# Norm sums of a GDN layer: from one row per head to one column per 128 tokens, and a page sum copied before the page loads are issued

## What is computed

```python
def l2norm(x):
    return x * lax.rsqrt(jnp.sum(x * x, axis=-1, keepdims=True) + EPS)
...
    q = l2norm(q.reshape(Bn, L, GDN_HEADS, GDN_DK)) * GDN_DK ** -0.5     # 4 heads of 128
    k = l2norm(k.reshape(Bn, L, GDN_HEADS, GDN_DK))
    o, S_new = run_chunks(gdn_chunk, S0, (q, k, v, g, beta), GDN_CHUNK)
    o = rmsnorm(o, norm_g) * jax.nn.silu(z)                              # per head of 128
...
    # fox_sample: softmax over 2048 past rows gathered by page_table, then
    jnp.einsum('bhqk,bkhd->bqhd', p[..., :P], vp)                        # the "page values"
```

## Time and profile before

| | us |
|---|---|
| median of 3 runs | 2619.35 (2618.45 to 2621.92) |
| the profiled execution | 2619.68 |
| its span, first to last instruction | 2617.9 |
| mean granted TensorE clock | 0.977 |

### The profile page before, as it was taken

How to read it: one execution, slowest core, us unless ns; L and a number is a source line. 1 busy time by engine, 2 the same in 40 slices (tenths; PEclk the granted TensorE clock), 3 DMA queues, 4 the chain that set the end, 5 groups by cost and what they waited for, 6 DMA issues and landing times.

```text
span 2617.9 us, 53417 instructions
## 1 busy us (share of the span) xinstructions
PE 2497.5 (95%) x20047; PEld 2395.9 (92%) x20047; DVE 1269.6 (48%) x2225; ACT 566.7 (22%) x847; POOL 1682.8 (64%) x750
## 2 busy tenths in 40 slices
PE   7999998997789899999999999999999899999997
PEld 7999998995467799999999999999889799999996
DVE  4444335786333564443344443366766644444433
ACT  3222101004633222220022220022222221222101
POOL 5777775663411377777777777765545457777773
PEclk9999999998789899999999999999999999999998
DMA  4333334894375333333323333233333423333331
GB/s 125 90 89 96 101 79 113 285 308 131 84 220 188 85 89 95 89 88 99 118 81 89 95 91 100 82 91 100 116 116 98 126 81 88 89 95 90 96 93 61
DMA packets 472390, 291.19 MB, mean 111 GB/s; under 512 B 32785, under 2 KB 438411, under 8 KB 472270
## 3 DMA queue, kind: packets, MB, share of 16 engines
q1 hardware_dynamic: 407286, 221.15, 29.0%
q10 hardware_dynamic: 64992, 68.54, 8.4%
HBM read 273.50 MB, written 16.23 MB: 111 GB/s over the span
## 4 chain that ended last, share of the span: by engine, by line
PE 83%; DVE 8%; ACT 3%; issue 3%; DMA 1%; POOL 1%; ACTq 1%; DVEq 0%; SPq 0%; POOLq 0%
PE ACC L799 72%; PE ACC L1055 2%; PE ACC L1028 1%; DVE TB L2261 1%; DMA SSR<-in_state_ret_S 1%; DVE SSR L2178 1%; POOL WLO L708 1%; PE ACC L1306 0%; PE ACC L1296 0%; DVE XL L1736 0%; PE ACC L1122 0%; PE ACC L1037 0%; POOL WHI L705 0%; PE ACC L893 0%; PE ACC L1330 0%
## 5 line engine op out<-in xcount | busy, mean ns | idle before, releaser
L705 POOL TENSOR_TENSOR WHI<-RAW,ZERO 128x1024 fp32r<-128x1024 f32 (+1 forms) x341 | 693.0, 2032 | 677.2 <-PE ACC L799 640.3
L708 POOL TENSOR_TENSOR WLO<-RAW,WHI 128x1024 fp32r<-128x1024 f32 (+1 forms) x341 | 915.5, 2685 | 49.3 <-POOL WHI L705 2.3
L799 PE MATMUL ACC<-XH,WHI 128*128 128x260 f32 x4032 | 822.6, 285 | 4.3 <-DVE XL L1736 2.0
L799 PE MATMUL ACC<-XH,WLO 128*128 128x260 f32 x4032 | 813.7, 283 | 0.0
L799 PE MATMUL ACC<-XL,WHI 128*128 128x260 f32 x4032 | 812.4, 283 | 0.0
L799 PEld LDWEIGHTS ACC<-XH,WHI 128*128 128x128 f32 x4032 | 624.8, 189 | 22.9 <-issue 6.5
L799 PEld LDWEIGHTS ACC<-XH,WLO 128*128 128x128 f32 x4032 | 622.9, 189 | 0.0
L799 PEld LDWEIGHTS ACC<-XL,WHI 128*128 128x128 f32 x4032 | 621.6, 189 | 0.0
L799 PE MATMUL ACC<-HH,WHI 128*128 128x260 f32 x1408 | 284.2, 283 | 1.1 <-POOL WLO L708 1.1
L799 PE MATMUL ACC<-HH,WLO 128*128 128x260 f32 x1408 | 283.1, 282 | 0.0
L799 PE MATMUL ACC<-HL,WHI 128*128 128x260 f32 x1408 | 282.6, 282 | 0.0
(11 more groups left out here) (391 smaller groups left out, 2398.7 us busy)
## 6 DMA issues: line engine op xcount, KB each, us to landing
RAW<-in_ffn_w_gu SPq DMA_DIRECT2D x176, 512.0 KB, 3.9
RAW<-in_ffn_w_down SPq DMA_DIRECT2D x64, 704.0 KB, 4.8
KPAGES<-in_cache_fox_k ACTq DMA_DIRECT2D x128, 256.0 KB, 4.1
RAW<-in_c_w_in SPq DMA_DIRECT2D x48, 512.0 KB, 3.9
VPAGES<-in_cache_fox_v SPq DMA_DIRECT2D x72, 256.0 KB, 3.1
RAW<-in_ab_w_in SPq DMA_DIRECT2D x28, 512.0 KB, 5.4
VPAGES<-in_cache_fox_v ACTq DMA_DIRECT2D x56, 256.0 KB, 3.3
SSR<-in_state_ret_S ACTq DMA_DIRECT2D x8, 1024.0 KB, 5.4
```

The source lines that it names most:

```text
L705: pool.tensor_tensor(WHI[:, slot, 0:nk, :], RAW[:, slot, 0:nk, :], ZERO[:, :].broadcast_to([P, nk, P]), ALU.add).then_inc(hi_split, 1)
L708: pool.tensor_tensor(WLO[:, slot, 0:nk, :], RAW[:, slot, 0:nk, :], WHI[:, slot, 0:nk, :].bitcast(F32), ALU.subtract).then_inc(split, 1)
L799: ins = pe.matmul(ACC[acc][:, n, 0:HALF], w[:, slot, k, :], a[:, k0 + k, n * HALF:(n + 1) * HALF], start=first and opens, stop=final and c ...
```

## The change

Sums of squares are formed per token. The squares become the weights (128 channels x 128 tokens) and one column of ones is the moving operand, so each matmul gives one column of 128 token sums. 520 tokens make five chunks, the fifth of which is the last 128 tokens (its last 8 are the samples). The result RN is 128 x 40 (8 heads x 5 chunks) for query and key and 128 x 20 for the output norm; root and reciprocal work on that. To come back to channels on partitions, one RN column is broadcast as 128 x 128 weights and multiplied with IDENT, six matmuls a head: 128, 128, 4, 124, 128 and 8 columns, since a chunk that crosses the 260-column halves is cut. ROWSEL and its two memsets go.

DVE instead of ACT squares the queries, before the last fox head's `lo`, and clears bank 7 there; ACT squares the keys in two parts and runs SiLU of values and gates after the roots instead of before. PE runs three of the four page-value turns before the sums. In pair 0 ACT copies page sum 1 before `sample_gates` and before four page loads that it issues, not after them; in both pairs PE runs the two `corner_xt` back to back ahead of the two page turns. KT1 and VT1 move in front of QS, and SQH takes the place from there on.

```diff
-        def row_select(r):
-            return ROWSEL[:, ROWSEL_ONE - r:ROWSEL_ONE - r + NORM_ROWS]
+        CHUNKS = NBLK + 1
+        RN = TA[:, 0:2 * CHUNKS * GDN_HEADS]
+        def chunk_tokens(c):
+            return slice(P * c, P * (c + 1)) if c < NBLK else slice(TOK - P, TOK)
+        def norm_column(c, j):
+            return CHUNKS * GDN_HEADS * (j // GDN_HEADS) + GDN_HEADS * c + j % GDN_HEADS
...
-            pe.wait_ge(fb_dve.sem, fb_dve.value("lo", FOX_HEADS - 1))
             pe.wait_ge(fs_dve.sem, fs_dve.value("norm"))
...
+            def token_sums(b, squares, j):
+                for c in range(CHUNKS):
+                    col = norm_column(c, j)
+                    ins = pe.matmul(bank(b)[:, col:col + 1], squares[:, j, chunk_tokens(c)], ONES[:, 0:1], start=True, stop=True)
+                return ins
+            def over_partitions(acc, j):
+                for c in range(NBLK):
+                    n, first = divmod(P * c, HALF)
+                    col = norm_column(c, j)
+                    left = RN[:, col:col + 1].broadcast_to([P, P])
+                    if first + P <= HALF:
+                        pe.matmul(acc[:, n, first:first + P], left, IDENT[:, :], start=True, stop=True)
+                    else:
+                        cut = HALF - first
+                        pe.matmul(acc[:, n, first:HALF], left, IDENT[:, 0:cut], start=True, stop=True)
+                        pe.matmul(acc[:, n + 1, 0:P - cut], left, IDENT[:, cut:P], start=True, stop=True)
+                n, first = divmod(SEQ, HALF)
+                col = norm_column(NBLK, j)
+                return pe.matmul(acc[:, n, first:first + DEC], RN[:, col:col + 1].broadcast_to([P, P]), IDENT[:, P - DEC:P], start=True, stop=True)
+            for _ in range(V_SLOTS - 1):
+                values()
+            pe.wait_ge(ln_dve.sem, ln_dve.value("sqq"))
             for j in range(2 * GDN_HEADS):
-                for n in range(2):
-                    ins = pe.matmul(ACC[0][0:NORM_ROWS, n, 0:HALF], row_select(r), SQH[:, j, n * HALF:(n + 1) * HALF],
-                                    start=j == 0, stop=j == 2 * GDN_HEADS - 1)
+                if j >= GDN_HEADS:
+                    pe.wait_ge(ln_act.sem, ln_act.value(f"sqk{(j - GDN_HEADS) // 2}"))
+                ins = token_sums(0, SQH, j)
             ln_pe.done(ins, "sum")
-            for _ in range(V_SLOTS):
-                values()
+            values()
+            pe.wait_ge(fb_dve.sem, fb_dve.value("lo", FOX_HEADS - 1))
             pe.wait_ge(ln_dve.sem, ln_dve.value("inv"))
             for j in range(2 * GDN_HEADS):
                 if j >= 2:
                     pe.wait_ge(ln_dve.sem, ln_dve.value(f"mul{j - 2}"))
-                for n in range(2):
-                    ins = pe.matmul(ACC[1 + j % 2][:, n, 0:HALF], IDENT[0:NORM_ROWS, r:r + 1].broadcast_to([NORM_ROWS, P]),
-                                    TA[0:NORM_ROWS, n * HALF:(n + 1) * HALF], start=True, stop=True)
-                ln_pe.done(ins, f"b{j}")
+                ln_pe.done(over_partitions(ACC[1 + j % 2], j), f"b{j}")
...
                 corner_xt(0)
+                corner_xt(1)
                 values()
-                corner_xt(1)
                 values()
...   (output norm: token_sums(0, SQO, j) and over_partitions(ACC[2 + j % 2], j) in the same way)
-            ln_act.done(act.activation(SQH[:, 0:GDN_HEADS, :], channels(GQ, GDN_HEADS), ACT.Square), "sqq")
-            ln_act.done(act.activation(SQH[:, GDN_HEADS:, :], channels(GK, GDN_HEADS), ACT.Square), "sqk")
+            for n in range(2):
+                ln_act.done(act.activation(SQH[:, GDN_HEADS + 2 * n:GDN_HEADS + 2 * n + 2, :], channels(GK + 2 * n, 2), ACT.Square), f"sqk{n}")
+            act.wait_ge(ln_pe.sem, ln_pe.value("sum"))
+            half = CHUNKS * GDN_HEADS
+            for first, c, scale, name in ((0, 1, float(P), "stdq"), (half, 0, 1.0, "stdk")):
+                ln_act.done(act.activation(RN[:, first:first + half], bank(0)[:, first:first + half], ACT.Sqrt, bias=EPSC[:, c:c + 1], scale=scale), name)
             act.wait_ge(cv_pool.sem, cv_pool.value("add3", CONV_CH - 1))
             act.activation(channels(GV, 2 * GDN_HEADS), channels(GV, 2 * GDN_HEADS), ACT.Silu).then_inc(cv_act, 1)
...
                     if p == 0 and n == LEVELS - 1:
+                        value_sum(1)
                         sample_gates()
...
                     if n > 1:
                         odd_values(V_PAIR * p + V_SLOTS + 2 * n + 3)
-                if p == 0:
-                    value_sum(1)
...
+                if h == FOX_HEADS - 1:
+                    dve.wait_ge(cv_act, 2)
+                    q = PRJ[:, GQ:GQ + GDN_HEADS, :]
+                    ln_dve.done(dve.tensor_tensor(SQH[:, 0:GDN_HEADS, :], q, q, ALU.mult), "sqq")
+                    await_step(dve, fa_act, "exp2", h)
+                    dve.memset(bank(7), 0.0).then_inc(v_clear, 1)
                 await_step(dve, fb_act, "hi", h)
                 fb_dve.done(dve.tensor_tensor(MOL[:, h, 0:SEQ], bank(VALUE_BANK), MOH[:, h, 0:SEQ].bitcast(F32), ALU.subtract), "lo")
-            dve.memset(bank(7), 0.0).then_inc(v_clear, 1)
             dve.wait_ge(ln_act.sem, ln_act.value("stdk"))
-            ln_dve.done(dve.reciprocal(TA[0:NORM_ROWS, :], TA[0:NORM_ROWS, :]), "inv")
+            ln_dve.done(dve.reciprocal(RN, RN), "inv")
```

More of the change, by code:

```diff
@@ L291, in trunk_program @@
         cursor["fp"] = cursor["fs"] = cursor["gd"] = cursor["abwork"]
+        KT1, VT1 = (new(n, [P, NBLK, P], area="fp") for n in ("KT1", "VT1"))
+        squares_at = cursor["fp"]
         QS = [new(f"QS{n}", [P, SEQ], area="fp") for n in range(2)]
-        KT1, VT1 = (new(n, [P, NBLK, P], area="fp") for n in ("KT1", "VT1"))
         KT, VT = ([t[:, 0:SEQ].rearrange("p (n d) -> p n d", n=NBLK), t1] for t, t1 in ((TA, KT1[:, :, :]), (TB, VT1[:, :, :])))
@@ L421, in trunk_program @@
         cv_act = sem("cv_act")
-        ln_act = Steps(sem("ln_act"), ["sqq", "sqk", "stdq", "stdk"])
+        ln_act = Steps(sem("ln_act"), ["sqk0", "sqk1", "stdq", "stdk"])
         ln_pe = Steps(sem("ln_pe"), ["sum"] + [f"b{j}" for j in range(2 * GDN_HEADS)])
-        ln_dve = Steps(sem("ln_dve"), ["inv"] + [f"mul{j}" for j in range(2 * GDN_HEADS)])
+        ln_dve = Steps(sem("ln_dve"), ["sqq", "inv"] + [f"mul{j}" for j in range(2 * GDN_HEADS)])
         both = range(2)
@@ L1223, in _ @@
             for j in range(GDN_HEADS):
-                for n in range(2):
-                    ins = pe.matmul(ACC[0][0:NORM_ROWS, n, 0:HALF], row_select(j), SQO[:, j, n * HALF:(n + 1) * HALF],
-                                    start=j == 0, stop=j == GDN_HEADS - 1)
+                ins = token_sums(0, SQO, j)
             go_pe.done(ins, "sum")
@@ L1232, in _ @@
                     pe.wait_ge(go_dve.sem, go_dve.value(f"norm{j - 2}"))
[L1233 to L1236, removed]
+                go_pe.done(over_partitions(ACC[2 + j % 2], j), f"b{j}")
             pe.wait_ge(fs_dve.sem, FOX_END)
@@ L1530, in _ @@
             act.wait_ge(cv_act, 4)
-            ln_act.done(act.activation(SQH[:, 0:GDN_HEADS, :], channels(GQ, GDN_HEADS), ACT.Square), "sqq")
-            ln_act.done(act.activation(SQH[:, GDN_HEADS:, :], channels(GK, GDN_HEADS), ACT.Square), "sqk")
+            for n in range(2):
[4 more added lines that the diff above has]
+                ln_act.done(act.activation(RN[:, first:first + half], bank(0)[:, first:first + half], ACT.Sqrt, bias=EPSC[:, c:c + 1], scale=scale), name)
             act.wait_ge(cv_pool.sem, cv_pool.value("add3", CONV_CH - 1))
             act.activation(channels(GV, 2 * GDN_HEADS), channels(GV, 2 * GDN_HEADS), ACT.Silu).then_inc(cv_act, 1)
-            act.wait_ge(ln_pe.sem, ln_pe.value("sum"))
-            for rows, c, scale, name in ((slice(0, 32), 1, float(P), "stdq"), (slice(32, NORM_ROWS), 0, 1.0, "stdk")):
-                ln_act.done(act.activation(halves(TA[rows, :]), ACC[0][rows, :, 0:HALF], ACT.Sqrt, bias=EPSC[rows, c:c + 1], scale=scale), name)
             act.wait_ge(ln_dve.sem, ln_dve.value(f"mul{2 * GDN_HEADS - 1}"))
@@ L1640, in _ @@
             act.wait_ge(go_pe.sem, go_pe.value("sum"))
-            go_act.done(act.activation(halves(TA[0:NORM_ROWS, :]), ACC[0][0:NORM_ROWS, :, 0:HALF], ACT.Sqrt,
-                                       bias=EPSC[0:NORM_ROWS, 0:1], scale=1.0 / P), "std")
+            half = CHUNKS * GDN_HEADS
+            go_act.done(act.activation(RN[:, 0:half], bank(0)[:, 0:half], ACT.Sqrt, bias=EPSC[:, 0:1], scale=1.0 / P), "std")
             act.wait_ge(go_dve.sem, go_dve.value("gate"))
@@ L2119, in _ @@
             dve.wait_ge(go_act.sem, go_act.value("std"))
-            go_dve.done(dve.reciprocal(TA[0:NORM_ROWS, :], TA[0:NORM_ROWS, :]), "inv")
+            go_dve.done(dve.reciprocal(RN[:, 0:CHUNKS * GDN_HEADS], RN[:, 0:CHUNKS * GDN_HEADS]), "inv")
             for j in range(GDN_HEADS):
```

12 lines of the change are left out of this document (1 added, 11 removed).

## The result

The changed kernel is slower: ratio 1.0074 to the kernel before, with a 95% interval from 1.0058 to 1.0090 (4 executions, median 2643.01 us, from 2637.38 to 2648.63; before 2620.01). The profiled execution took 2637.38 us, 17.7 more than the profiled one of before; 2634.5 had been forecast.

What follows compares the result with a forecast made beforehand. The prediction took PE, with 83% of the chain, its short hand-offs and its changing clock to bound the kernel; 15.2 - 4.4 + 0.25 + 3.8 = +14.9 on 2619.7 gave 2634.5 us, range 2619 to 2641.

Steps and rivals of the forecast that it cites:

- What one instruction costs: PE's float32 matmuls: two instructions each, 0.11 us at 2.4 GHz or 0.213 at 1.2, whatever moves below 128 columns.
- Query and key sums: First norm on PE: 80 instructions replace 10.03 us, clock falling inside them; 13.7 us, ending at 707.1.
- Root and reciprocal: Between first-norm sums and spreading: 0.9 us with hand-offs, covered by the fourth page turn; spreading starts at 709.0.
- Spreading: First norm's broadcast on PE: clock stays low, 2.56 us a head, 20.5 for eight; `mul7` +15.2 us.
- the rival: Clock comes back during the first norm's spreading: 13.1 us instead of 20.5, +7.8 there, total +4.5; chance 0.20.
- The squares: Query squares on DVE before the last fox head ends: ready by 686.0, bank 7 by 686.5, costing nothing.
- the rival of late squares: DVE's squares come late behind POOL: +3 us on the forecast, 2637.5; chance 0.06.
- Page sum 1: Pair 0, copy ahead of four page loads: PE's whole 4.46 us stall goes, -4.4 us; pair 1 +0.25.
- The rival by which removing the stall gains nothing: Pair 0: PE's turn waits next for ACT or a page, giving 2639 us; chance 0.07.
- Output norm: Sums 8.5 us and spreading 10.25 at low clock, +3.3; with 0.5 for chunks ahead of `lo`, +3.8 us.
- The other side: Clock holds through sums and spreading: first norm -0.2, output norm -5.7, total -11, 2608 us; chance 0.11.

Runs made afterwards that it cites:

- norms_alone: Changed kernel with the page sum copy and the corners of pair 0 put back as before; ratio 1.0070 to the kernel before.
- the edit alone: Kernel before with only page sum 1 copied ahead of the page loads and both corners ahead of the turns; ratio 0.9987 to the kernel before.
- wide_sums: Changed kernel with 128 moving columns of ones instead of one in every norm sum, same instruction count; ratio 0.9966 to the kernel before.
- turns_late: Changed kernel with the three page turns moved back behind the query and key sums; ratio 1.0025 to the kernel before.
- fewer_wide: Changed kernel with 128-column sums and fewer instructions, four heads' last 8 tokens sharing one sum and one spreading; ratio 1.0005 to the kernel before.

## Why the prediction was right, point by point

- **What one instruction costs.** Right. 0.11 us at 2.4 GHz and 0.213 at 1.2, taken from a matmul of four columns, is what single columns cost (4.5 us for 41 records; 17.07 for 80), and 128 columns cost 0.115.
- **Query and key sums.** Foretold 13.7 us with the clock falling inside them; measured 12.7 to 12.9 in the four profiles with single columns behind the page turns. The fast part lasted 4.5 us and not 3.5, the only error. The turns ended at 692.9 (693.4 foretold).
- **Root and reciprocal.** 0.9 us under the fourth turn, as foretold; spreading began at 707.4 (709.0).
- **Spreading.** 2.56 us a head at 0.50, as foretold, 20.65 in both profiles of the changed kernel; `mul7` +13.8 instead of +15.2, the difference being mostly that of the sums (from the fox head's end it is +13.2 in both profiles). The choice between low and returning clock was the least certain step, and norms_alone shows that it could have gone the other way: there it rose after 7.2 us, `mul7` at +7.5, where the rival had foretold +7.8. That both profiles of the changed kernel fell on the forecast's side is in part luck.
- **The squares.** Ready at 685.5 and bank 7 at 686.1 (686.0 and 686.5 foretold): nothing lost, and the rival of late squares falls. The wait of 1.3 us behind POOL did not come, though: the products took 2.53 us with all waiting, 0.2 over the 2.33 of the sum, and began 0.6 later.
- **Page sum 1.** The whole stall went: -4.9 between `mul7` and `u` (-4.4 foretold), 4.8 in the edit alone. In the second profile of the changed kernel it is -3.1: no stall there either, but PE loses 1.0 us on the way to 766 us, not traced further, and 0.8 at the end of the pair, where the clock falls earlier. The rival by which removing the stall gains nothing falls.
- **Output norm.** Under-sized: +3.5 up to `lo` (3.3 foretold), then 1.5 where 0.5 had been allowed; 5.0 instead of 3.8, the upper bound. The reason given for the 0.5 was not the one: the four chunks ahead of `lo` were done 4.1 us before it. The loss lies behind `lo`, where the clock, back at 1.00 before PE's idle wait, was down again.
- **The other side.** The clock did not hold, but wide_sums makes that rival's case, and its sizes were nearly right for the first norm: 9.2 and 10.85 us against 8.9 and 10.7, first GDN matmul 0.25 us before that of before, -0.2 foretold. Over the output norm it gave less than the -5.7 foretold, its sums being at 0.68. The prediction weighed the Trainium skill's rule (TensorE: Matmul & The Clock Gate, Part 1), that sustained matmul activity releases the throttle, against L1218's fall. For single columns the measurement disagrees with the rule: PE was busy without a pause for 12.7 us and lost its clock in the middle. For 128 columns it agrees.

Adding up, +13.8 - 4.9 + 0.2 + 3.5 + 1.5 = +14.1 at the end of the stage; +14.9 had been foretold. What was not foreseen at all is what lies behind it: 3.5 us of retention layer in one profile and -2.0 in the next, and executions of one kernel that differ by 11 us. The sum had taken every stage without an edit as unchanged.

## What to carry to other kernels

Price a float32 matmul of few columns with weights of its own by its two instructions, here 0.11 us each at full clock, not by its columns, and count how many instructions an elegant reformulation issues; here 80 and 96 took the place of 32 and 32. Then ask what clock they will get: in this kernel a run of instructions that moved next to nothing lost TensorE's clock although the engine was busy throughout, and what stood behind it paid. Moving 128 columns instead of one, or putting wide matmuls between two narrow runs, cost next to nothing and gave back 0.4 to 1% of the whole kernel. And where two engines start within 0.1 us of each other on a shared port, a stage that ends earlier can be paid for in a later one: compare the stages' ends, not only the totals.

## What the runs showed that had not been expected

- Doing 128 times the work in the sums made the kernel 0.9 to 1.1% faster than the changed one (0.9966 against 1.0061 and 1.0074).
- A narrow spreading keeps a clock that it finds up (10.85 us in wide_sums, 10.88 in turns_late) and mostly doesn't bring back one that it finds down (20.65 twice, 14.45 once).
- 0.06 us between the starts of a DVE product and a POOL split decide over 1.7 us of that product, 2.2 us of a state load; with the count of late products the rest of the span went from 1721 to 1736 us.
- 14 to 16 us won between the fox head and `lo` (fewer_wide) were worth nothing in the ratio until one product was moved 1.4 us ahead in another layer; with it the kernel is at 0.9963, level with wide_sums (0.9966). Both beat the kernel before as well as the changed one.
